# Three-block transformer forward pass: 512-column high-weight matmuls in 256-feature blocks, and relative-bias rows stored without a copy for each partition

## The reference

```python
def odd_layer(x, norm_g, w_in, q_gain, k_gain, sinks, w_out, rel_bias):
    h = rms_norm(x, norm_g) @ w_in
    q, k, v, gate = split_cols(h, ODD_SPLITS)
    ...
    o = swa_sink_attention(q, k, v, sinks, rel_bias)
    return x + (jax.nn.silu(gate) * o) @ w_out

# second_block, after the branches
x = x + (g_a * y_a + g_b * y_b + g_c * y_c) @ w_out[l]
h = rms_norm_2(x, norm_mlp_g[l])
x = x + jnp.square(jax.nn.relu(h @ w_mlp_up[l])) @ w_mlp_down[l]
```

## Time and profile before

| | |
|---|---|
| median of 3 runs (lowest to highest) | 2600.68 us (2598.48 to 2601.88) |
| span of the profiled execution, first to last instruction | 2598.5 us |
| TensorE busy (matmul) | 2446.8 us, 94% of the span |
| VectorE, ScalarE, GpSimd busy | 1433.4, 1064.9, 128.6 us |
| mean granted TensorE clock | 0.969 of 2.4 GHz |
| chain of work that ended last: TensorE, DMA, VectorE, ScalarE | 82%, 8%, 5%, 3% |
| DMA traffic | 436.5 MB, 168 GB/s |

### The profile page before, as it was taken

How to read it: one execution, slowest core, us unless ns; L and a number is a source line. 1 busy time by engine, 2 the same in 40 slices (tenths; PEclk the granted TensorE clock), 3 DMA queues, 4 the chain that set the end, 5 groups by cost and what they waited for, 6 DMA issues and landing times.

```text
span 2598.5 us, 48560 instructions
## 1 busy us (share of the span) xinstructions
PE 2446.8 (94%) x19832; PEld 2419.2 (93%) x19832; DVE 1433.4 (55%) x1666; ACT 1064.9 (41%) x1333; POOL 128.6 (5%) x113
## 2 busy tenths in 40 slices
PE   7676699999988899999999999999999999999997
PEld 7576589999988899999999999999999999999997
DVE  6242466566645564457775455555654554554554
ACT  4121255444545443343654444444443343333342
POOL 0000130110000110000000000001100000000001
PEclk9787799999989999999999999999999999999999
DMA  6767644554433355545555555555555555555553
GB/s 194 131 128 129 153 149 149 185 178 155 148 113 117 126 203 193 176 150 171 171 195 186 181 184 183 174 191 182 172 189 185 185 180 185 182 183 186 180 186 114
DMA packets 126601, 436.51 MB, mean 168 GB/s; under 512 B 20575, under 2 KB 20831, under 8 KB 126440
## 3 DMA queue, kind: packets, MB, share of 16 engines
q1 hardware_dynamic: 113472, 413.19, 48.2%
q0 software_dynamic: 11872, 18.44, 5.1%
q10 hardware_dynamic: 1096, 2.49, 0.3%
HBM read 420.88 MB, written 13.11 MB: 167 GB/s over the span
## 4 chain that ended last, share of the span: by engine, by line
PE 82%; DMA 8%; DVE 5%; ACT 3%; issue 1%; ACTq 0%; SPq 0%; DVEq 0%
PE GP L374 26%; PE GP L376 26%; PE GP L375 26%; DMA RAW<-w_dram 8%; DVE WL L1001 2%; ACT WH L704 1%; PE OP L489 1%; PE PT L455 1%; PE LOG L473 1%; DVE HL L1054 1%; ACT HH L725 0%; PE PT L608 0%; DMA X<-x_dram 0%; PE LOG L548 0%; DVE S L1025 0%
## 5 line engine op out<-in xcount | busy, mean ns | idle before, releaser
L1001 DVE TENSOR_TENSOR WL<-RAW,WH 128x1024 fp32r<-128x1024 f32 x784 | 961.1, 1234 | 1060.6 <-ACT WH L704 1057.5
L704 ACT ACTIVATE WH<-RAW 128x1024 fp32r<-128x1024 f32 x784 | 822.4, 1056 | 1278.9 <-PE GP L376 1060.3
L374 PE MATMUL GP<-HH,WH 128*128 128x256 f32 x4064 | 1178.3, 290 | 59.6 <-DVE WL L1001 59.6
L375 PE MATMUL GP<-HL,WH 128*128 128x256 f32 x4064 | 1166.0, 287 | 0.0
L376 PE MATMUL GP<-HH,WL 128*128 128x256 f32 x4064 | 1165.3, 287 | 0.0
L374 PEld LDWEIGHTS GP<-HH,WH 128*128 128x128 f32 x4064 | 797.3, 196 | 69.9 <-DVE WL L1001 41.5
L375 PEld LDWEIGHTS GP<-HL,WH 128*128 128x128 f32 x4064 | 797.3, 196 | 0.1
L376 PEld LDWEIGHTS GP<-HH,WL 128*128 128x128 f32 x4064 | 796.4, 196 | 0.0
L374 PE MATMUL GP<-GH,WH 128*128 128x256 f32 x2064 | 587.3, 285 | 7.3 <-DVE GL L1062 3.7
L375 PE MATMUL GP<-GL,WH 128*128 128x256 f32 x2064 | 585.8, 284 | 0.0
L376 PE MATMUL GP<-GH,WL 128*128 128x256 f32 x2064 | 585.8, 284 | 0.0
(11 more groups left out here) (218 smaller groups left out, 1084.0 us busy)
## 6 DMA issues: line engine op xcount, KB each, us to landing
RAW<-w_dram SPq DMA_DIRECT2D x784, 512.0 KB, 3.7
bias_rows<-ROWS_SB POOLq DMA_DIRECT2D x14, 768.0 KB, 32.2
B<-bias_rows POOLq DMA_DIRECT2D x14, 512.0 KB, 4.5
X<-x_dram ACTq DMA_DIRECT2D x4, 512.0 KB, 10.2
y_dram<-S SPq DMA_DIRECT2D x4, 512.0 KB, 2.6
ONEHOT<-onehot_dram ACTq DMA_DIRECT2D x1, 148.5 KB
small<-small_dram ACTq DMA_DIRECT2D x1, 130.0 KB, 3.9
ident<-const_dram ACTq DMA_DIRECT2D x1, 64.0 KB
```

The lines of the kernel that those rows point to most:

```text
L374: pe.matmul(o, wh, rh, start=start, stop=False, skip_group_check=True)
L375: pe.matmul(o, wh, rl, start=False, stop=False, skip_group_check=True)
L704: act.activation(WH[:, slot], RAW[:, slot], ACT.Copy).then_inc(hi_ready, 1)
L1001: dve.tensor_tensor(WL[:, slot], RAW[:, slot], WH[:, slot].bitcast(F32), ALU.subtract)\
```

## The change

**Matmuls.** The high and low halves of an activation tile lie side by side in one array (H2 for HH and HL, G2, SC2, XC2 in the same way). `two` multiplies the high weights by both halves in one matmul of 512 columns, whose output is one PSUM bank: high sums in its first half, high-by-low sums in its second. The low weights are multiplied by the high half, 256 columns, into the second half of the bank. So a weight tile takes 2 matmuls with 768 columns in all, where it took 3 with 768. `gemm_pair`, the two pool subs and the two gate subs keep the three matmuls: 36 subs; 748 subs change.

**Blocks.** A feature tile now fills a bank, so a block is 2 feature tiles (256 features) from 4 subs of 4 input tiles each. The weights' order in DRAM follows. To take a block out, ScalarE copies the second halves from PSUM to LO (128 x 512; it waits for the block's last sub and for the block before it to be out), VectorE adds LO to the first halves (`whole`), waits for itself, and multiplies by the norm. There are 151 such blocks. Residual blocks have no LO: VectorE does two adds, one after the other. In the MLP ScalarE squares twice (to GH and to UU) instead of copying once. In the mix stage a round is a block of 4 subs and one of 2. Waits on counts of blocks are renumbered; some now name a later or an earlier point by half an old block. A layer's first block waits for the normalized activations every sub, so for the last 4 tiles before its fourth sub.

**Bias rows.** `bias_rows` holds 56 rows of 384 numbers, once. Three stores write it, of 16, 32 and 8 rows, with no wait on the subs, and the first two loads follow at once. The rows are made in the opposite direction, the load skews by starting one place further for each partition, and L1104's successor reads B backwards along the keys.

```diff
-            def three(o, wh, wl, rh, rl, start, stop):
-                pe.matmul(o, wh, rh, start=start, stop=False, skip_group_check=True)
-                pe.matmul(o, wh, rl, start=False, stop=False, skip_group_check=True)
-                return pe.matmul(o, wl, rh, start=False, stop=stop, skip_group_check=True)
+            def two(o, wh, wl, r2, start, stop):
+                if stop:
+                    pe.matmul(o[:, 1, :], wl, r2[:, 0, :], start=False, stop=False, skip_group_check=True)
+                    return pe.matmul(o, wh, r2, start=False, stop=True, skip_group_check=True)
+                pe.matmul(o, wh, r2, start=start, stop=False, skip_group_check=True)
+                return pe.matmul(o[:, 1, :], wl, r2[:, 0, :], start=False, stop=False, skip_group_check=True)
...
-            def gemm(RH, RL, nkt=NT, k0=0, kts=2, n_out=4, ready=None, tick=None):
-                ps = open_block()
-                for j in range(nkt // kts):
-                    if ready is not None and (j * kts) % 4 == 0:
-                        pe.wait_ge(ready[0], ready[1] + (j * kts) // 4 + 1)
+            def gemm(R2, nkt=NT, k0=0, ready=None, tick=None):
+                ps = halves_of(open_block())
+                for j in range(nkt // 4):
+                    if ready is not None:
+                        done, before, step = ready
+                        pe.wait_ge(done, before + step * (j + 1))
...
-            def block_splits(tick=None):
-                splits(8, tick)
+            def block_splits(tick=None, subs=4):
+                splits(subs, tick)
+                act.wait_ge(subs_used, used.add(subs))
+                if blk.base:
+                    act.wait_ge(psum_free, blk.value)
+                blk.add()
+                act.activation(LO[:, :, :], halves_of(blk.base - 1)[:, :, 1, :], ACT.Copy).then_inc(lo_taken, 1)
...
+            def whole(dst, n=4):
+                used.add(n)
+                dve.wait_ge(lo_taken, lo.add())
+                blk.add()
+                return dve.tensor_tensor(dst, halves_of(blk.base - 1)[:, :, 0, :], LO[:, :, :], ALU.add)
...
             def times_rs(dst):
-                ps = block_done()
-                for k in (0, 2):
-                    ins = dve.tensor_tensor(dst(k), ps[:, k:k + 2], rs_of(2), ALU.mult)
-                ins.then_inc(psum_free, 1)
+                step(whole(dst))
+                dve.tensor_tensor(dst, dst, rs_of(2), ALU.mult).then_inc(psum_free, 1)
...
-                                    scalar=scale(4 * chunk + h, qt), in1=B[:, gc % 2, h, T - nk:T],
+                                    scalar=scale(4 * chunk + h, qt), in1=B[:, gc % 2, h, nk - 1::-1],
...
             def hidden_hi(t0):
-                act.wait_ge(hidden_ready, hidden.add())
-                act.activation(GH[:, bass.ds(t0, 4), :], UU, ACT.Copy).then_inc(gh_ready, 1)
+                act.wait_ge(psum_free, blk.value)
+                act.activation(GH[:, bass.ds(t0, 2), :], UT, ACT.Square)
+                act.activation(UU, UT, ACT.Square).then_inc(gh_ready, 1)
...
-                    src = bass.AP(bias_rows, (a.row0 + 4 * chunk) * bias_head + P - 1,
-                                  [[ROWS, P], [bias_head, 4], [1, T]])
+                    src = bass.AP(bias_rows, (a.row0 + 4 * chunk) * ROWS, [[1, P], [ROWS, 4], [1, T]])
...
-                for gc in chunks:
-                    pool.wait_ge(subs_used, 10 + 3 * gc)
-                    a = MOBA if 4 * gc >= MOBA.row0 else SWA if 4 * gc >= SWA.row0 else DSA
-                    r = slice(4 * gc - a.row0, 4 * gc - a.row0 + 4)
-                    pool.dma_start(bias_rows.ap()[4 * gc:4 * gc + 4, :, 0:ROWS],
-                                   ROWS_SB[r, (DSA, SWA, MOBA).index(a), None, :].to_broadcast([4, P, ROWS]))\
-                        .then_inc(rows_stored, 16)
+            for k, a in enumerate((DSA, SWA, MOBA)):
+                pool.dma_start(bias_rows.ap()[a.row0:a.row0 + a.heads, :], ROWS_SB[0:a.heads, k, :])\
+                    .then_inc(rows_stored, 16)
+            pool.wait_ge(rows_stored, 16 * 3)
+            load_biases(DSA, (0, 1))
             pool.wait_ge(score_ready, 1)
```

More of the change, by code:

```diff
@@ L410, in gemm, with gemm_pair @@
                         tick(j)
-            def gemm_pair(RH, RL, tiles, waits, tick):
+            def gemm_pair(R2, tiles, waits, tick):
                 halves, n = [], 0
@@ L434, in gemm_pair, with gemms @@
                         n += 1
-            def gemms(n, RH, RL):
-                with loop(pe, n, [(sub, 4 * AHEAD), (blk, 2)]):
-                    for _ in range(2):
-                        gemm(RH, RL)
+            def gemms(n, R2):
+                with loop(pe, n, [(sub, 4 * AHEAD), (blk, 4)]):
+                    for _ in range(4):
+                        gemm(R2)
             def ssq(n):
@@ L693, in _ @@
             raw = [Count(raw_full[k]) for k in range(AHEAD)]
-            gr, var, mix, hidden = Count(gate_ready), Count(var_ready), Count(mix_ready), Count(hidden_ready)
-            rounds = [(sub, 16), (blk, 2)] + [(c, 16 * 4) for c in raw]
+            gr, var, mix, used = Count(gate_ready), Count(var_ready), Count(mix_ready), Count(subs_used)
+            rounds = [(sub, 16), (blk, 4), (used, 16)] + [(c, 16 * 4) for c in raw]
             def splits(n, tick=None):
@@ L789, in _ @@
                 act.activation(S[:, 16 + 4 * n:20 + 4 * n, :], X[:, t, :], ACT.Square).then_inc(sq0_ready, 1)
[L792 to L793 removed]
+            block_splits()
             token_root()
@@ L867, in _ @@
             token_root()
-            block_splits()
+            for b in range(3):
+                block_splits()
             with loop(act, 2, rounds):
-                for _ in range(2):
+                for _ in range(4):
                     block_splits()
@@ L941, in _ @@
                 last = branch == 2
-                steps = [(sub, 24), (blk, 4)] + [(c, 16 * 6) for c in raw] + [(mix, 2)] * last
-                with loop(act, 2, steps) as i:
+                steps = [(sub, 12), (blk, 4), (used, 12)] + [(c, 16 * 3) for c in raw] + [(mix, 2)] * last
+                with loop(act, 4, steps) as i:
                     for b in range(2):
@@ L992, in _ @@
             hh, gh, gr, steps_n = Count(hh_ready), Count(gh_ready), Count(gate_ready), Count(dve_step)
-            std = Count(std_ready)
-            rounds = [(sub, 16), (used, 16), (blk, 2)]
+            std, lo = Count(std_ready), Count(lo_taken)
+            adds = [(sub, 16), (used, 16), (blk, 4), (steps_n, 4)]
+            rounds = adds + [(lo, 4)]
             def splits(n, tick=None):
@@ L1467, in _ @@
                 if g < 3:
-                    with loop(dve, 2, rounds) as i:
-                        for b in range(2):
-                            splits(8)
-                            add_residual(8 * i + 4 * b)
-            for b in range(4):
-                splits(min(8, n_subs - sub.base))
-                add_residual(4 * b)
+                    with loop(dve, 2, adds) as i:
+                        for b in range(4):
+                            splits(4)
+                            add_residual(8 * i + 2 * b)
@@ L1475, in _ @@
+            for b in range(8):
+                splits(min(4, n_subs - sub.base))
+                add_residual(2 * b)
             token_norm(4)
```

424 lines of the change are left out of this document (221 added, 203 removed).

## The result

The changed kernel takes 2444.39 us (median of 4 runs, 2441.38 to 2446.99), the kernel before beside it 2599.63 (2598.48 to 2601.88). The ratio is 0.940, with a 95% interval of 0.9387 to 0.9414. 155 us are gone, where 180 were forecast. The profiled execution has a span of 2440.6 us and a time of 2442.34.

The account below looks back on a forecast made before the run. Bounds: TensorE's matmul spacing late, weight transfers held by bias stores in the first stretch. 2598.5 - 111 - 4.5 - 72.1 + 8 = 2418.9 us of span, plus 2.2 for the median: 2421 us, range 2350 to 2510.

Parts of the forecast that it names:

- The bias rows: First stretch, 62 to 316 us: without the large stores 42 subs take 143 us, gain 111 us (76 to 121).
- the loads of B and the backward read: Skewed bias loads and reversed reading on VectorE: taken as 0 us, though the read could be 0 to 46 us of VectorE's time.
- The price of the wide matmul: On TensorE, 13.3 ns come once per matmul, so a wide and narrow pair costs 346.7 ns against 360; chance 0.45.
- The three rivals on the price: Pair at 360 ns (cost by column), 2498 us, chance 0.20; 336 ns, 2360 us, 0.14; 327 ns, 2308 us, 0.12.
- The 72.1 + 4.5 us: Gain of wide matmuls at 13.3 ns a pair: 72.1 us outside the first stretch, 4.5 us inside it.
- The added work: LO copies and extra VectorE steps hidden in steady state; 8 us lost at layer boundaries and beside attention steps.
- 3 beside the attention steps: Loss from denser engine queues beside the attention steps: 3 us (0 to 10).
- the 5 at the layer boundaries: TensorE waits 1.2 us at each of three layer boundaries, a little more at the first hidden block: 5 us (0 to 10).
- the quarter taken off there: DSA and SWA stretches, 93 subs: three quarters of 9.9 us counted, 7.4, since TensorE is not always the late one.
- its slower rival: 512 columns cannot be fed at full rate: 547 ns a pair, +1119 us, 3610 in all; chance 0.02.
- the stores are not the cause: Bias stores do not hold the weights, so the first stretch's rounds stay and only 72 us are gained: 2537 us; chance 0.03.
- the late evacuation chain: ScalarE waits at LO for TensorE, losing half a microsecond in each of 151 blocks, 75 us: 2496 us; chance 0.04.

Follow-up runs that it names:

- the bursts: Twelve bursts of 32 matmuls or pairs added at the end of the changed kernel: 120 ns for 256 fp32r columns, 227 for 512, 346.8 a pair.
- the store runs: Kernel with the matmul part and old 14 bias stores, stores reading from 128 or 32 partitions instead of 4: 2445.02, 2444.32, 2442.97, 2443.53 us.

## Why the prediction was right, and where it was not

The time, 2444.4 us, lies in the range of 2350 to 2510, 23 us over the forecast. Step by step:

- **The bias rows: right, a little low.** Forecast 111 us (with the old matmuls); 118.7 measured by the part alone. The working put the 42 subs at 143 us, 10 of them for steps that wait on each other. With the bias part alone 42 subs take 138 us from 62 us on; when sub 60 is split the lead over before is 116.5 us, at sub 210 it is 119.4. So some 5 us of the surplus are there by the end of the first stretch and some 3 come in the attention stages. That the loads of B and the backward read are free was right: the successor of L1104 has 408 ns in the middle of its 96 against 410.
- **The price of the wide matmul: right as a mechanism.** The 13.3 ns do come once per matmul, and the pair alone costs 346.8 ns. The three rivals on the price fall with the bursts.
- **The 72.1 + 4.5 us: the term that was mis-sized.** It multiplied the 13.3 by every pair. Measured are 44.2 us (the wide matmul split again), because most blocks stand at 353.2: 7425 / 2 pairs by 6.4 ns are 24 us, and a share of the 1040 pairs in broken groups is up to 7 us more, of the 32 that are missing. No row of before could show the second spacing. It lies at the very edge of the prediction's own bound for a pair, 340 to 353 ns.
- **The added work: right.** Forecast 8 us, measured 7.4 by the medians (4.2 by the profiled executions, below). The boundary waits are there, 3 of up to 1.2 us. LO copies have 0.58 us and no wait before them.

By stretches of the weight stream (start of the split of the sub named, from ScalarE's timeline), for the kernel with the bias part alone, the one with the wide matmul split again, and after. The gain of the wide matmul is the third column less the fourth, the added work the third less the second.

| subs | bias part alone, us | wide matmul split, us | after, us | gain of the wide matmul (forecast) | added work |
|---|---|---|---|---|---|
| 0 to 60 | 208.9 | 208.0 | 205.6 | 2.4 (5.0) | -0.9 |
| 60 to 210 | 573.0 | 575.6 | 571.4 | 4.2 (10.2) | 2.6 |
| 210 to the end | 1697.2 | 1699.7 | 1663.6 | 36.1 (61.4) | 2.5 |
| all | 2479.1 | 2483.3 | 2440.6 | 42.7 (76.6) | 4.2 of 8 |

The gain is four to six tenths of the forecast in every stretch. Were every pair at 353.2 ns, 6.8 under 360 and not 13.3, the three forecasts would be 2.6, 5.2 and 31.4 us, an estimate from the spacing alone; the late stretch has more, since part of it stands at 347. In the attention stretches (60 to 210) 1.6 us are gained in all. The prediction has 10.2 there, less 3 beside the attention steps and a part of the 5 at the layer boundaries; measured are 4.2 and 2.6, so both are smaller, and that the difference comes out near is luck. Whether the quarter taken off there, for TensorE not always being the late one, was right can't be read from this.

The total is closer than its terms. The 32 us that the matmuls fell short are partly made good by the 8 that the bias rows gave beyond their forecast, and that is luck too. One sum of the prediction has a slip that changes nothing: its slower rival comes to 2498 + 1119 = 3617 us, not 3610.

Of the rivals, that the stores are not the cause falls with the store runs, the late evacuation chain with 7.4 us for all that was added, and the slower case with the bursts.

## What to carry to other kernels

Price a matmul as its columns plus a constant per instruction, and measure the constant for your type: it decides whether merging matmuls pays (13.3 ns for fp32r at 256 columns here, some 3 for bfloat16). Then time the whole sequence too, since the sum of the single prices gave nearly twice the gain that was measured here. Where wide and narrow matmuls alternate, look at the distance of starts in several blocks and try an order in which equals stand together. A store that broadcasts from a few partitions can hold up the transfers on another queue; let it read from many (32 were enough here, as the outermost size), or don't store the copies.

## What was not expected of the hardware

- The same sequence of instructions has two steady spacings, 346.6 and 353.2 ns a pair, the second as a cycle of 361, 349 and 350. Which one holds depends on the matmuls before it, and it can last over tens of blocks; wide, wide, narrow, narrow stands at 348.3 each time.
- fp32r has a constant of 13 to 15 ns per matmul at 256, 384 and 512 columns, bfloat16 about 3, and 128 columns of fp32r take 110 ns, as 256 columns of bfloat16 do.
- A store of 768 KB from 4 partitions took 26.6 us and made 512 KB loads on another queue take 22.2 in place of 3.3; from 32 or 128 partitions it took 7.0 or 5.2, and the loads 5.8 or 4.3, which cost the kernel nothing. Its packets of 4,608 bytes took 725, 295 and 200 ns with 4, 32 and 128 source partitions.
